# Four stages of a two-layer streaming encoder kernel re-ordered at once: modulation load, first latent pair, sample latents, first pool tiles

## The reference, cut to what matters

```
mod = silu(c) @ w_ada + b_ada                    # shift, scale, gate for each layer, one vector per sequence
h   = rmsnorm(x) * (1 + scale) + shift
# layer 0: z = h @ w_in gives q, k, v (differential heads), cq, ckv, kpe (latent heads) and a gate
q_nope, q_pe = cq @ w_uq, rope(cq @ w_uqr);  q_lat = q_nope @ w_uk
logits = (q_lat . ckv_all + q_pe . kpe_all) * scale;  o_b = (softmax(logits) @ ckv_all) @ w_uv    # 8 latent heads
x = x + gate * ((concat(o_a, o_b) * silu(g)) @ w_out)
# layer 1: u, g = split(h @ w_in_pool); d = trailing mean of u over 2/4/8/16 rows - u; a linear map per channel group
x = x + gate * ((m * silu(g)) @ w_out_pool);  y = rmsnorm(x)
```

## Time and profile before

| | us |
|---|---|
| median of three runs (lowest, highest) | 2052.51 (2049.96, 2053.9) |
| the profiled execution | 2055.45 |
| its span, first to last instruction | 2053.6 |
| PE busy | 1880.6 |
| DVE busy | 1199.4 |
| ACT busy | 401.1 |

### The profile page before, as it was taken

The page is one execution under the profiler, slowest core; times in us unless marked ns, Lnnn a source line. Parts: engine busy times, 40 slices in busy tenths (PEclk is TensorE's granted clock), DMA queues, the critical chain, the costliest instruction groups (busy, mean ns, idle before and its releaser), DMA issues.

```text
span 2053.6 us, 32904 instructions
## 1 busy us (share of the span) xinstructions
PE 1880.6 (92%) x13314; PEld 1721.4 (84%) x13314; DVE 1199.4 (58%) x1589; ACT 401.1 (20%) x884; POOL 117.9 (6%) x93
## 2 busy tenths in 40 slices
PE   4889999999999989998888899958999999999995
PEld 2239999999999977776777779958999999999995
DVE  3738667766976654552455544377777544574444
ACT  2121000000000112331455543440000000121111
POOL 2000000000600000000000011200000000001110
PEclk9999999999999999998799998979999999999997
DMA  9765545555654431204333254214545332552222
GB/s 385 293 228 182 203 185 191 201 210 210 223 213 186 170 114 52 78 22 154 99 115 116 90 193 142 92 41 166 185 185 194 117 121 103 179 186 82 82 82 87
DMA packets 86251, 316.08 MB, mean 154 GB/s; under 512 B 12200, under 2 KB 20568, under 8 KB 60464
## 3 DMA queue, kind: packets, MB, share of 16 engines
q1 hardware_dynamic: 63200, 229.31, 31.0%
q10 hardware_dynamic: 21200, 76.48, 10.3%
q0 software_dynamic: 1792, 9.49, 1.2%
HBM read 282.56 MB, written 32.69 MB: 154 GB/s over the span
## 4 chain that ended last, share of the span: by engine, by line
PE 69%; DVE 13%; DMA 8%; issue 5%; ACT 5%; SPq 0%; DVEq 0%; ACTq 0%; POOL 0%; POOLq 0%
PE banks L719 68%; DMA w_adr<-in_w_ada_dve 4%; DMA w_raw<-in_w_pin 3%; DVE banks L1633 2%; ACT pxd L1410 1%; DVE std L1881 1%; DVE w_hi L1592 1%; DMA d_raw<-pool_d_scratch 1%; DVE rstd L1572 1%; DVE x L2082 1%; DVE pt_lo L1815 0%; ACT px L1328 0%; DVE w_hi L1865 0%; DVE stage L2048 0%; DMA w_raw<-in_w_out 0%
## 5 line engine op out<-in xcount | busy, mean ns | idle before, releaser
L719 PE MATMUL banks<-h_hi,w_hi 128*128 128x272 f32 x3968 | 830.7, 295 | 57.5 <-DVE w_lo L1593 20.1
L719 PE MATMUL banks<-h_lo,w_hi 128*128 128x272 f32 x3712 | 776.8, 291 | 0.0
L719 PE MATMUL banks<-h_hi,w_lo 128*128 128x272 f32 x3456 | 721.7, 291 | 0.0
L719 PEld LDWEIGHTS banks<-h_hi,w_hi 128*128 128x128 f32 x3968 | 634.0, 193 | 68.6 <-issue 46.2
L719 PEld LDWEIGHTS banks<-h_lo,w_hi 128*128 128x128 f32 x3712 | 594.8, 192 | 0.0
L719 PEld LDWEIGHTS banks<-h_hi,w_lo 128*128 128x128 f32 x3456 | 546.2, 191 | 0.0
L1633 DVE CUSTOM_DVE_ANT_0 banks<-w_adr,cond_b 128x2048 f32<-128x2048 f32 x144 | 335.2, 2328 | 29.2 <-DMA w_adr<-in_w_ada_dve 26.6
L1592 DVE CAST w_hi<-w_raw 128x2048 fp32r<-128x2048 f32 x100 | 124.5, 1245 | 223.2 <-PE banks L719 171.2
L1593 DVE TENSOR_TENSOR w_lo<-w_raw,w_hi 128x2048 fp32r<-128x2048 f32 x100 | 246.9, 2469 | 3.5
L1265 ACT ACTIVATE stage<-banks 128x544 f32<-128x544 f32 x46 | 28.9, 628 | 496.3 <-PE banks L719 496.3
L1973 DVE TENSOR_TENSOR x<-x,stage 128x544 f32 (+1 forms) x32 | 24.0, 749 | 169.4 <-ACT stage L1492 169.4
(11 more groups left out here) (308 smaller groups left out, 1614.6 us busy)
## 6 DMA issues: line engine op xcount, KB each, us to landing
w_adr<-in_w_ada_dve ACTq DMA_DIRECT2D x46, 1024.0 KB, 5.1
w_raw<-in_w_z SPq DMA_DIRECT2D x32, 1024.0 KB, 6.9
w_raw<-in_w_pin SPq DMA_DIRECT2D x32, 1024.0 KB, 5.8
w_more<-in_w_ada_pe SPq DMA_DIRECT2D x19, 1024.0 KB, 7.1
w_adr<-in_w_ada_dve SPq DMA_DIRECT2D x18, 1024.0 KB, 4.9
w_raw<-in_w_gate SPq DMA_DIRECT2D x16, 1024.0 KB, 6.7
w_raw<-in_w_out SPq DMA_DIRECT2D x32, 512.0 KB, 3.9
w_raw<-in_w_pout SPq DMA_DIRECT2D x16, 1024.0 KB, 4.9
```

The lines of the kernel that those rows point to most:

```text
L719: return pe.matmul(out, lhsT, rhs, start=start, stop=stop)
```

## The change

Four stages are edited, and the buffers that this needs are laid out anew.

1. Start. `ADA_PE` 24 to 20, `ADA_P0` 8 to 12: PE computes the shift blocks and four scale blocks, DVE twelve scale blocks. All these loads go through SP, alternating, with four slots for the DVE tiles; x comes later in the queue. ACT, not DVE, adds the bias to the turned results.
2. First latent pair. Its items use banks 2 to 7 in turn, with looser waits; the rotation of `kpe` moves behind item 1.
3. Sample latents. They run inside the last pair, after units 24 to 32; their cache loads are issued after the last item.
4. Pool layer. The split of the second pool tile moves ahead of the row sums, both first tiles run block by block of h, and `silu(cond_b)` moves ahead; DVE's splits run one tile ahead (`G_PIN + 2`, `G_PIN + 3`), and SP alternates ada load and weight load. In the group stage the splits move to the end of each group.

```diff
-ADA_PE = 24
-ADA_P0 = 8
+ADA_PE = 20
+ADA_P0 = 12
-PE_MOD = (KT + 8, KT + 12, 0, 4, 8, 12)
+PE_MOD = (KT + 12, 0, 4, 8, 12)
...
+            load_piece(0)
+            load_scale(0)
+            load_piece(1)
+            load_scale(1)
+            load_scale(2)
+            sp.dma_start(x[:, 0:KT // 2], xT[:, 0:KT // 2]).then_inc(x_in, 16)
+            load_piece(2)
+            load_scale(3)
+            sp.dma_start(x[:, KT // 2:KT], xT[:, KT // 2:KT]).then_inc(x_rest_in, 16)
+            load_piece(3)
+            load_scale(4)
+            load_scale(5)
+            for g in range(4, 10):
+                load_piece(g)
+                load_scale(g + 2)
+            for g in range(10, ADA_PE):
+                load_piece(g)
...
+            pair = 2 if t else (2, 4, 6, 2, 2, 4, 6, 6, 2)[k]
+        FIRST_EV = (0, 0, 0, 1, 1, 3, 3, 3, 4)
...
             sp.wait_ge(ml_item, ITEMS * (HEADS // 2))
-            sp.wait_ge(ml_score, ML_UNITS - 7)
             sp.dma_start(ccT[:], ckvT.rearrange("(c p) k -> p c k", p=P)).then_inc(ms_in, 16)
-            sp.dma_start(ccR[:], ckv.rearrange("(k p) c -> p k c", p=P)).then_inc(ms_in, 16)
+            sp.wait_ge(ml_score, ML_UNITS - 8)
             for e in range(2):
                 sp.dma_start(kpc[64 * e:64 * e + 64, :], kpeT).then_inc(ms_in, 16)
+            sp.dma_start(ccR[:], ckv.rearrange("(k p) c -> p k c", p=P)).then_inc(ms_in, 16)
+            sp.wait_ge(ml_pv, HEADS - 2)
...
+                if w == ML_UNITS - 8:
+                    samp_keys()
+                for g, w0 in enumerate((ML_UNITS - 7, ML_UNITS - 4)):
+                    if w == w0:
+                        samp_scores(g)
+                    if w == w0 + 1:
+                        samp_turn(g)
+                    if w == w0 + 2:
+                        samp_values(g)
+                if w == ML_UNITS:
+                    samp_out()
...
+            for s in range(2):
+                load_w(w_pin[s], (G_PIN + s) % 2, G_PIN - G_KPE + s)
             with sp.Fori(0, KT // 2) as t:
-                for s in range(2):
-                    load_w(tile_of(wp2, s, t), (G_PIN + s) % 2, 2 * t + G_PIN - G_KPE + s)
                 for s in range(2):
                     sp.wait_ge(adr_used, 2 * t + (ADA_P0 + ADA_P1 + s))
                     sp.dma_start(w_adr[:, 1], tile_of(wd2, s, t + (ADA_P0 + ADA_P1) // 2)).then_inc(adr_in[s], 16)
+                    load_w(tile_of(wp2, s, t + 1), (G_PIN + s) % 2, 2 * t + G_PIN + 2 - G_KPE + s)
...
-                big_tile((G_PIN + s) % 2, KT)
+            for k in range(KT):
+                pe.wait_ge(h_ready, KT + k + 3)
+                for s in range(2):
+                    m = tile_products((G_PIN + s) % 2, k, k == 0, k == KT - 1)
...
             fold_scale(1)
+            split(G_PIN + 1)
             row_var(1)
...
-                    split(G_PIN + 1, dve_t2, t)
+                    split(G_PIN + 2, dve_t2, t)
...
-                    split(G_PIN + 2, dve_t2, t)
+                    split(G_PIN + 3, dve_t2, t)
```

More of the change, by code:

```diff
@@ L148, in program @@
         over_raw.close()
+        over_val = ExitStack()
+        wva = sb("wva", [P, LT, HEADS * P], scope=over_val)
+        over_val.close()
         over_half = ExitStack()
@@ L317, in program @@
         ring_in = [sem(f"ring_in{i}") for i in range(RING)]
[L318 removed]
+        scale_in = [sem(f"scale_in{s}") for s in range(4)]
         adr_in = [sem(f"adr_in{s}") for s in range(2)]
@@ L677, in _ @@
             pool.dma_start(lam_in[:], lamv.to_broadcast((P, 4 * DQK)).rearrange("p (a d) -> p a d", a=4)).then_inc(consts_in, 16)
-            for a in range(2, ADA_P0):
-                pool.wait_ge(adr_used, a - 1)
-                load_ada(a)
             pool.wait_ge(mq_in, 32)
@@ L917, in values, with samp_keys, samp_scores @@
                          pt_hi[:, s], pt_lo[:, s]).then_inc(ml_pv, 1)
+            def samp_keys():
+                pe.wait_ge(ml_ev, ITEMS * (HEADS // 2))
+                for c in range(LT):
+                    m = pe.transpose(PS[0:NS, 3, c * P:(c + 1) * P], ckT[:, c, NP:R], id_t[:])
+                m.then_inc(ms_mm, 1)
+            def samp_scores(g):
+                if g == 0:
+                    pe.wait_ge(ms_in, 64)
+                pe.wait_ge(ms_act, S_VALUE_EV[0] if g else S_KEYS_EV)
+                heads = slice(4 * g, 4 * g + 4)
+                old, new = slice(0, PAST - HALF), slice(PAST - HALF, HALF)
+                for bank, cols, keys_c, keys_p in (
+                        (2, slice(0, HALF), lambda c: ccT[:, c, 0:HALF], kpc[:, 0:HALF]),
+                        (3, old, lambda c: ccT[:, c, HALF:PAST], kpc[:, HALF:PAST]),
+                        (3, new, lambda c: ckT[:, c, NP:R], kpe[:, NP:R])):
+                    for c in range(LT):
+                        small(PS[:, bank, cols], qls[:, c, heads, :].rearrange("p h r -> p (h r)"), keys_c(c), c == 0, False)
+                    m = small(PS[:, bank, cols], qps[:, heads, :].rearrange("p h r -> p (h r)"), keys_p, False, True)
+                m.then_inc(ms_mm, 1)
@@ L1501, in _ @@
                 gated(t, G_O2, 1, 2 * KT, halves=True)
+            act.wait_ge(condb_in, 32)
+            act.activation(cond_b[:], cond_b[:], ACT.Silu).then_inc(condb_ready, 1)
             with act.Fori(KT // 2 - 1, KT // 2) as t:
@@ L1505, in _ @@
             affine1()
-            act.wait_ge(condb_in, 32)
-            act.activation(cond_b[:], cond_b[:], ACT.Silu).then_inc(condb_ready, 1)
             act.wait_ge(pad_zero, 1)
```

364 lines of the change are left out of this document (186 added, 178 removed).

## The result

The changed kernel takes 2070.0 us in the median of 5 runs (2068.33 to 2075.17), the kernel before 2053.9 beside it (2049.96 to 2056.81): a ratio of 1.0085, 95% interval 1.0066 to 1.0104. It is some 16 us slower. The forecast was 4.7 us slower, 2057.2 us, with a range of its own of 2048 to 2067 and 2043 to 2070 over all cases.

A forecast was written before the change was run, and what follows sets the result against it. PE was taken as the bound, so stages gain only where it idles or runs at the lower clock. Terms -22 - 11 + 10 + 26.7 + 1 = +4.7 on the median 2052.51 gave 2057.2 us, range 2048 to 2067 (2043 to 2070 over all cases).

The forecast's parts named there:

- Part 4, the pool loop: Pool layer: 17 us gained ahead, then every split waits for its weight load, 16.0 us per tile; +26.7 us in all.
- the group stage: Group stage: one more split between the last tile and `lower_d`, partly covered; +1 us, ends 0 and +3.5.
- Part 1, the start: Start: DVE paces, z tiles start at 139.4 instead of 161.6 us; -22 us, ends -17 and -26.
- Part 2: First latent pair: with six banks every item finds its banks free, idle time goes; -11 us, ends -8.7 and -12.
- Part 3: Sample latents inside the last pair: cache loads, hand-overs and clock cost more than the filled idle time; +10 us.
- the `w_out` halves: Behind the last latent head: `w_out` loads issued only at `ml_fin`, no longer covered by sample work; 8 us exposed.
- (a): Pool loop keeps its pace because a weight load is in time after all; 2016.5 us, chance 10%.
- (b): Sample latents in the last pair cost nothing, products at 2.4 GHz and loads landing sooner; 2047 us, chance 17%.
- (c): Start: one load queue delivers less or first z tile waits on PE; fifth tile 6 us later, 2063 us, 10%.
- (d): First latent pair: six banks do not close it up, DVE's chain holds the evictions; 2068 us, chance 3%.
- the signs named: Trace signs for the forecast: z tiles, first scores, cache-load wait, `w_out` wait, 16 waiting splits with tiles 15 to 16.5 us apart.

The follow-up runs named there:

- part 1 alone: The kernel before with only the start changed (twelve DVE tiles, one load queue): 2038.2 us, ratio 0.9915.
- Experiment 8: Changed kernel with x later in the start's load queue: both halves behind DVE's sixth tile, 2078.5 us; then only the second half behind the fifth, 2074.2 us.
- Experiment 6: Changed kernel with both groups of sample latents one unit later in the last latent pair: 2079.7 us, ratio 1.0127.
- experiment 1: Changed kernel with the weight load ahead of the wait for `adr_used` and the ada load in SP's pool loop: 2013.8 us, ratio 0.9797.

## Why the prediction was right in its sign and wrong in its size

The sign was forecast, but with a chance of 45%: the sum of +4.7 was hardly more than the 4.1 us that a measurement can tell. What failed is the size, by 12.8 us in the median (2070.0 against 2057.2): the time from `adr_used` to the landed weight load in the pool loop was taken too short, and two terms of the start were mis-sized.

**Part 4, the pool loop: the mechanism right, the term 8 us too small.** The working took 7.6 us from `adr_used` to the landed weight load, 0.2 to the issue, 4.9 for an ada load and 1.05 MB at 400 GB/s (which add to 7.7), though the row of before for the same pair, named beside it, gave 8.1. In the changed kernel it took 7.5 us in one turn (1388.0 to 1395.46) and 8.8 in the next (1403.8 to 1412.58), the longer ones with the stores of `pool_d_scratch` and `pool_gate_scratch` beside them. So a tile took 245.7 / 15 = 16.38 us instead of the 15.9 of the forecast: +7.2. The tiles behind it took 12.15 instead of 12.04, the group stage 2.1 instead of 1; the third tile came 41.3 us after the row sums, where 42.3 were forecast. This is what the +8.8 of part 4 and the group stage are made of. With the row's 8.1 a tile takes 16.4 in the same sum, +34.2, and +34.4 was measured; 7.6 gave +26.7: where a reckoned time and a row of the same pair of loads differ, the row should carry the sum. The loop turned where it was forecast to, after 245.7 us: the last gap of PE is ahead of 1611.77.

**Part 1, the start: -17.3 where -22 was forecast**, at the end of its own range (-17). Two steps failed. The fifth DVE tile started at 45.7, not 43.5: 388 GB/s over 45.7 us are 17.7 MB, almost a tile more than the 16.8 counted, since some of what was queued behind it had moved as well; the rate of 400 was not the fault, as the window of the changed kernel shows.

```profile
20.00:40.00 20.00, 11.26 (x37) 7.30 (x36) 15.10 (x16) 4.92 (x8) 0.00 (x0) 0.83 1.01 426
```

The Trainium skill gives two figures here, about 358 GB/s for one core on the page "DMA: Bandwidth & Descriptors", section "Specifications", and some 120% of that for a core alone on the page "Perfetto Trace Analysis", section "Roofline"; the trace, with 426, agrees with the second.

Then two pieces and three quarters of a tile took 19.3 us from 115.07 to 134.4, not 16.2, because PE came to them after idle time and ran the first of them at the lower clock: a mean of 0.87 in that window. The working priced every product of the start at full clock. Experiment 8 sizes this: with 1.2 us of idle time ahead of the first product the same work took 17.0 us, so 2.3 of the 3.1 are the clock and 0.8 a sum too short. Its z tiles start at 139.2, and the forecast said 139.4; that is in part luck, since its fifth DVE tile started at 40.7, 2.8 us earlier than the forecast had it. The baseline moves too: the old start took 161.6 in the trace of before, 157.9 to 163.3 in others, and part 1 alone gave -15 in the median.

**Part 2: right.** First product of the pair to first scores 28.3 us (723.67 to 751.98) instead of 39.9, -11.6 against -11 forecast; up to the last pair it is -12.9, of which 1.2 are the z and gate tiles, and -14 alone.

**Part 3: right in size, its prices less so.** +11.8 in the profile, +13 alone and +13 in the whole, against +10 with ends +1 and +17. The wait for the cache loads was 6.99 us (forecast 7). The last head was done 81.9 us after the pair's first scores, where 79.6 were forecast. From the last step on the sample latents (`ms_fin`) to the first differential maximum it took 14.2 us instead of 6.3, so 7.9 exposed, where 8 were forecast; but the load that PE waited for was `vds`, 9.8 us, and the `w_out` halves that the working named cost 1.0:

```profile
969.77 1.87 PE L1035 MATMUL banks<-id_t,vds 128*32 128x128 f32 x8 [9.79 <-DMA vds<-out_z]
```

The clock was taken as one price (990 between 984 and 995.6), but it differs from one execution to the next: 0.77 or 0.70 in this stretch. Over the traces the price of part 3 runs from 12 to 20 us, so that the closeness of +11.8 to the forecast is in part luck, it being the low end; the medians gave +13. Experiment 6 shows that idle time taken out there need not shorten it. The Trainium skill, page "TensorE: Matmul & The Clock Gate", section "HAM oscillation — how this bites in real kernels", tells of bursts between waits that run at the lower clock again and again; the same eight value products that took 1.16 us in one execution and 2.08 in the other agree with it.

**The rivals.** (a), the loop keeps its pace, would have given 2016.5: it fell as the loop stands, and the kernel of experiment 1, where the weight load is in time, gave 2013.8. (b), part 3 costs nothing, fell. (c), the fifth tile lands later, was true by 2.2 us, not by its mechanism, the rate. (d) fell.

Of the signs named, the pool loop's and the wait for the cache load (6.99 us) came as described, with 15 waiting splits for 16. The z tiles, 144.3, missed 139 +/- 4, and the `w_out` product was not held for 7 to 9 us by a load of its own.

The stretches add up: -17.3 - 12.9 + 11.8 - 3.5 + 34.4 + 2.1 = +14.6, the difference of the spans. Of the 9.9 us between this and the forecast, part 4 with the group stage holds 8.8, the start 4.7 and part 3 1.8; part 2 (-1.9) and the differential stage (-3.5) go the other way. The other 2.9 of the 12.8 us between the medians are the profiled execution of before, which was 2.9 us slower than the median to which the difference was added.

What stays open: why the clock in the last pair is lower in one execution than in another, and with the samples one unit later; and how small a gain at the start the total keeps.

## What to carry to other kernels

When a load is moved behind another on one queue, ask what releases each of the two: the load that the next step waits for belongs ahead of any wait for something it doesn't need. Here one line moved by two places took off 56 us, where the four parts together had added 16. Where a row shows the very pair of loads that a sum needs, take its time rather than one built of a landing and a rate. And judge edits of under 5 us stage by stage in the trace, between two events that both kernels have, since stages with short products and short waits spread by as much from one execution to the next.

## What the runs showed of the hardware that was not expected

The same instructions in the last pair, behind the same waits, took 96.0 us at a mean granted clock of 0.77 and 101.4 at 0.70 in two executions of one program, while the pool loop took 245.7 in both. Taking 5 us of DMA wait out of the last pair did not make it shorter: 103.4 us at 0.65. A 1 MB load landed 4.8 us after its issue with none ahead of it on its queue, 5.1 us with one of 128 KB ahead and 7.3 with one of 1 MB (medians of the pool loops). After 3.8 us of idle time at the start PE took 19.3 us for products that took 17.0 after 1.2 us. The core moved 426 GB/s over 20 us of the start.
